# Where the operands of the dense products begin in SBUF: rows without a pad, tensors at multiples of 512 bytes

## The reference, cut to what matters

```python
def first_block(x, mem, ...):
    u = rms_norm(h, g_mix[l]) @ w_in[l]          # then two kinds of attention
    ...
    h = h + y @ w_out[l]
    h = h + cross_attention(rms_norm(h, g_cross[l]), rms_norm(mem, g_mem[l]), ...)
    a = jnp.square(jax.nn.relu(rms_norm(h, g_mlp[l]) @ w_up[l]))
    h = h + a @ w_down[l]

def _shift(z):
    return jnp.pad(z, ((0, 0), (1, 0), (0, 0)))[:, :-1]

def _rwkv7_mixer(h, r, k, v, mu_w, mu_a, w0, w1, w2, a0, a1, a2, ...):
    h_prev = _shift(h)                            # token t sees token t-1; token 0 sees zeros
    xw = h + (h_prev - h) * mu_w
    xa = h + (h_prev - h) * mu_a
    w = -jax.nn.softplus(-(w0 + jnp.tanh(xw @ w1) @ w2)...) - 0.5
    a = jax.nn.sigmoid((a0 + (xa @ a1) @ a2)...)
```

## The kernel before

| operand | begins at (before) | steps from row to row | begins at (after) |
|---|---|---|---|
| h, row k | 32 + 32 k | 4128 | 0 |
| u, row k | 288 + 32 k | 4128 | 0 |
| y, row k | 0 | 4096 | 0 |
| ul and hid in arena, row k | 384 | 4096 | 0 |
| w_hi, w_lo, part k | 0 | 512 | 0 |

## Time and profile before

### The profile page before, as it was taken

How to read it: one execution, slowest core, us unless ns; L and a number is a source line. 1 busy time by engine, 2 the same in 40 slices (tenths; PEclk the granted TensorE clock), 3 DMA queues, 4 the chain that set the end, 5 groups by cost and what they waited for, 6 DMA issues and landing times.

```text
span 2386.9 us, 35554 instructions
## 1 busy us (share of the span) xinstructions
PE 2287.9 (96%) x14900; PEld 1784.5 (75%) x14900; DVE 1176.7 (49%) x1498; ACT 866.1 (36%) x1524; POOL 546.9 (23%) x244
## 2 busy tenths in 40 slices
PE   7999999998999999999999999999999999999997
PEld 4777766666787877778888888888676777778885
DVE  6777746768565554532122122123416566467654
ACT  4444357767444222231121131133325422354321
POOL 2322212121211222222222222222131133222221
PEclk9999999999999999999999999999999999999999
DMA  3211101113131100111111111112221011100022
GB/s 129 79 45 53 54 27 36 54 45 124 62 124 45 35 28 27 44 44 53 45 44 53 44 48 49 44 53 80 80 69 31 18 36 37 46 18 13 4 107 80
DMA packets 37279, 125.88 MB, mean 53 GB/s; under 512 B 3856, under 2 KB 4368, under 8 KB 36752
## 3 DMA queue, kind: packets, MB, share of 16 engines
q1 hardware_dynamic: 30864, 103.30, 13.4%
q10 hardware_dynamic: 6272, 20.49, 2.3%
HBM read 114.34 MB, written 8.91 MB: 52 GB/s over the span
## 4 chain that ended last, share of the span: by engine, by line
PE 84%; DVE 9%; ACT 5%; issue 2%; DMA 1%; ACTq 0%; DVEq 0%
PE PS L182 22%; PE PS L184 21%; PE PS L183 21%; PE PS L2012 2%; PE PS L748 1%; PE PS L771 1%; PE PS L1196 1%; PE PS L898 1%; PE PS L933 1%; PE PS L915 1%; DVE arena L1017 1%; PE PS L316 1%; PE PS L1633 1%; DVE arena L397 1%; PE PS L1493 1%
## 5 line engine op out<-in xcount | busy, mean ns | idle before, releaser
L182 PE MATMUL PS<-u_r,w_hi 128*128 128x512 f32 x1280 | 522.7, 408 | 18.0 <-DVE y_r L192 5.4
L184 PE MATMUL PS<-u_r,w_lo 128*128 128x512 f32 x1280 | 507.3, 396 | 0.0
L192 POOL TENSOR_TENSOR w_lo<-w_raw,w_hi 128x1024 fp32r<-128x1024 f32 x143 | 364.1, 2546 | 587.4 <-ACT w_hi L188 581.4
L183 PE MATMUL PS<-arena_r,w_hi 128*128 128x512 f32 (+1 forms) x1152 | 439.4, 381 | 0.0
L231 POOL TENSOR_TENSOR w_hi<-w_raw,const 128x1024 fp32r<-128x1024 f32 x77 | 153.1, 1989 | 1143.3 <-PE PS L182 1093.8
L182 PEld LDWEIGHTS PS<-u_r,w_hi 128*128 128x128 f32 x1280 | 241.7, 189 | 82.8 <-DVE arena_r L192 6.5
L184 PEld LDWEIGHTS PS<-u_r,w_lo 128*128 128x128 f32 x1280 | 241.6, 189 | 57.4
L183 PEld LDWEIGHTS PS<-arena_r,w_hi 128*128 128x128 f32 x1152 | 216.9, 188 | 43.1 <-issue 0.7
L182 PE MATMUL PS<-h_r,w_hi 128*128 128x512 f32 x512 | 210.5, 411 | 4.0 <-DVE u_r L405 3.7
L184 PE MATMUL PS<-h_r,w_lo 128*128 128x512 f32 x512 | 202.9, 396 | 0.0
L183 PE MATMUL PS<-y_r,w_hi 128*128 128x512 f32 x512 | 202.0, 395 | 0.0
(11 more groups left out here) (399 smaller groups left out, 3573.0 us busy)
## 6 DMA issues: line engine op xcount, KB each, us to landing
w_raw<-in_w SPq DMA_DIRECT2D x174, 512.0 KB, 3.5
arena<-in_w SPq DMA_DIRECT2D x10, 512.0 KB, 4.7
h<-in_xT ACTq DMA_DIRECT2D x1, 4096.0 KB, 15.4
u<-parked_stream ACTq DMA_DIRECT2D x1, 4096.0 KB, 13.0
out<-arena SPq DMA_DIRECT2D x16, 256.0 KB, 2.0
parked_stream<-h ACTq DMA_DIRECT2D x6, 512.0 KB, 2.6
h<-in_xT SPq DMA_DIRECT2D x8, 256.0 KB, 7.3
h<-in_xT ACTq DMA_DIRECT2D x8, 256.0 KB, 9.1
```

The source lines that it names most:

```text
L182: first = pe.matmul(out, a[0], b[0], start=start, stop=False)
L183: pe.matmul(out, a[0], b[1], start=False, stop=False)
L184: return first, pe.matmul(out, a[1], b[0], start=False, stop=stop)
L192: return e.tensor_tensor(out, x, hi_part.bitcast(F), ALU.subtract)
```

## The change

Rows of h and u lose the pad and are 1024 words. h, u, y and arena are placed at multiples of 512 bytes; `small` and `ada` move behind arena. The shifted product of the first half of the tokens is cut in two: its first two columns are streamed from a small new tensor `edge` (two parts, high and low; 8 rows of two words, a zero and token 0), and the other 510 columns from h and u, words 1 to 510 of the row, into columns 2 to 511 of the bank. DVE fills `edge` ahead of its other work in `wa_dve`; PE waits for it. The two clearing instructions at the start go.

```diff
-        def with_rounded(name, shape):
+        def with_rounded(name, shape, align=512):
...
-            t = ctx.enter_context(nc.sbuf_tensor(name, shape, F, align_bytes=64))
+            t = ctx.enter_context(nc.sbuf_tensor(name, shape, F, align_bytes=align))
...
-        h_all, h_r = with_rounded("h", [P, KC, PAD + T])
-        u_all, u_r = with_rounded("u", [P, KC, PAD + T])
+        h_all, h_r = with_rounded("h", [P, KC, T])
+        u_all, u_r = with_rounded("u", [P, KC, T])
...
-        small = sb("small", [P, 64])
-        ada = sb("ada", [P, 24])
...
         arena, arena_r = arena_t[:, :], arena_rt[:, :]
+        small = sb("small", [P, 64])
+        ada = sb("ada", [P, 24])
+        edge = sb("edge", [P, 2, KC, 2], R)
...
         def in_u(k, lo, hi):
-            return u_r[:, k, PAD + lo:PAD + hi]
+            return u_r[:, k, lo:hi]
...
         def lora_down_pe(pe, h):
...
             if h == 0:
                 pe.wait_ge(S("gl_y_ready"), 1)
+                pe.wait_ge(S("edge_ready"), 2)
...
                 product(pe, bank(0), (rest_hi[:, k, :], rest_lo[:, k, :]), u_two(k, lo, hi), k == 0, False)
-                m = product(pe, bank(0), (mu_hi[:, k, :], mu_lo[:, k, :]), u_two(k, lo - 1, hi - 1), False, k == KC - 1)[1]
+                mu = (mu_hi[:, k, :], mu_lo[:, k, :])
+                if h == 0:
+                    product(pe, bank(0)[:, 0:2], mu, (edge[:, 0, k, :], edge[:, 1, k, :]), False, False)
+                    m = product(pe, bank(0)[:, 2:HALF], mu, u_two(k, 1, hi - 1), False, k == KC - 1)[1]
+                else:
+                    m = product(pe, bank(0), mu, u_two(k, lo - 1, hi - 1), False, k == KC - 1)[1]
...
         def wa_dve(dve):
+            dve.wait_ge(*split_ready("u2"))
+            dve.memset(edge[:, :, :, :].bitcast(F), 0.0).then_inc(S("edge_clear"), 1)
+            dve.wait_ge(S("edge_clear"), 1)
+            for x, source in enumerate((h_r, u_r)):
+                dve.tensor_copy(edge[:, x, :, 1:2], source[:, :, 0:1].bitcast(F)).then_inc(S("edge_ready"), 1)
             dve.wait_ge(S("wa_in"), 32)
...
-            dve.memset(u_r[:, :, 0:PAD].bitcast(F), 0.0)
-            dve.memset(h_r[:, :, 0:PAD].bitcast(F), 0.0)
...
-            act.dma_start(uT[:, :, PAD:], park_d[:, 0:KC, :]).then_inc(S("parked"), 16)
+            act.dma_start(uT, park_d[:, 0:KC, :]).then_inc(S("parked"), 16)
```

More of the change, by code:

```diff
@@ L147, in vcol @@
             return vec[:, VEC[name][0] + j:VEC[name][0] + j + 1]
-        h_all, h_r = with_rounded("h", [P, KC, PAD + T])
-        u_all, u_r = with_rounded("u", [P, KC, PAD + T])
+        h_all, h_r = with_rounded("h", [P, KC, T])
+        u_all, u_r = with_rounded("u", [P, KC, T])
         y_all, y_r = with_rounded("y", [P, KC, T])
-        hT, uT, yT = h_all[:, :, PAD:PAD + T], u_all[:, :, :], y_all[:, :, :]
+        hT, uT, yT = h_all[:, :, :], u_all[:, :, :], y_all[:, :, :]
         NS = 4
@@ L161, in program @@
         arena, arena_r = arena_t[:, :], arena_rt[:, :]
+        small = sb("small", [P, 64])
+        ada = sb("ada", [P, 24])
+        edge = sb("edge", [P, 2, KC, 2], R)
         def U(k, lo=0, hi=T):
-            return uT[:, k, PAD + lo:PAD + hi]
+            return uT[:, k, lo:hi]
         def pair(high, low):
@@ L170, in in_u @@
         def in_u(k, lo, hi):
-            return u_r[:, k, PAD + lo:PAD + hi]
+            return u_r[:, k, lo:hi]
         def in_h(k, lo, hi):
-            return h_r[:, k, PAD + lo:PAD + hi]
+            return h_r[:, k, lo:hi]
         def in_y(k, lo, hi):
@@ L2763, in _ @@
             pre = (in_(hT), lambda k: gpre[:, k:k + 1], f_rs, "fin")
-            u2 = (in_(uT[:, :, PAD:]), in_h, in_u, pre, lambda k: ada[:, k:k + 1])
+            u2 = (in_(uT), in_h, in_u, pre, lambda k: ada[:, k:k + 1])
             for q in range(14):
@@ L2988, in u2_split @@
             def u2_split(h, ks):
-                split_act(act, "u2", h, in_(uT[:, :, PAD:]), in_h, lambda k: [norm_out("fin", k, h)], ks, shift=lambda k: ada[:, k:k + 1])
+                split_act(act, "u2", h, in_(uT), in_h, lambda k: [norm_out("fin", k, h)], ks, shift=lambda k: ada[:, k:k + 1])
             for q in range(14):
```

## The result

| | before | after |
|---|---|---|
| median of the runs beside each other (4 and 4) | 2395.94 us | 2367.98 us |
| lowest and highest | 2384.31 to 2396.93 | 2366.30 to 2374.37 |
| ratio, with 95% interval | | 0.9889 (0.9873 to 0.9904) |
| profiled execution, span | 2386.9 us | 2372.6 us |
| its time | not recorded | 2374.37 us |

The kernel became some 27 us faster (1.1%; 0.0111 x 2395.9 = 26.6 by the ratio, 23 to 30 by its interval, 28.0 between the medians); 17.5 had been forecast, 2379 us, in a range of 2363 to 2399. The profiled execution of after is the slowest of its four; only 1.8 us of its time lie outside the span.

What follows compares the result with a forecast made beforehand. The prediction took PE's matmul spacing to bound the kernel: MLP -10.2, other products -9.7, edge matmuls +2.4, together -17.5 us from the 2396.3 us median, giving 2379 us, in a range of 2363 to 2399 us.

Steps and rivals of the forecast that it cites:

- What bounds the kernel, and the cause: PE, busy 96% of the span; distance between operands' beginnings sets matmul spacing, with a floor of 226.7 ns.
- Rival 1: Everywhere: beginnings don't matter, so only the edge matmuls' +2.4 us is left, 2399 us; chance 0.11.
- rival 3: All streams: in step is the bad place, 395 ns a matmul, 19.7 us slower, 2416 us; chance 0.07.
- MLP, -10.2 us: Four up stages each 1.70 us and four down stages each 0.84 us shorter, all on the path.
- The other products, -9.7 us: Outside the MLP, 4080 wide matmuls: 2720 gain 4.3 ns each, 11.7 us, of which 9.7 on the path.
- 0.83: Share of the products outside the MLP taken to lie on the path, 821 / 987, giving 9.7 of 11.7 us.
- Rival 2: Outside the MLP nothing gains, as only long runs settle: -10.2 + 2.4 = -7.8 us, 2388 us; chance 0.18.
- Settling: In product pieces, spacing comes down to the floor only after some matmuls; 8 of every 24 spent on it.
- The edge matmuls, +2.4 us: 24 two-column matmuls on PE, priced at 0.098 us each from a one-column row with the same weight load.
- pieces whose first third is uneven: Sign of being right, outside the MLP: a piece's first third is uneven and its rest even.
- DVE and the transfers, nothing: DVE's small instructions fall in idle time, PE's wait for edge is over early, u's reload is covered: no cost.
- The sum: -10.2 - 9.7 + 2.4 = -17.5 us on the 2386.9 us span; median 9.4 us above it carried over: 2379 us.

Runs made afterwards that it cites:

- the second and the third: Profiles of the changed kernel run again unchanged: medians 2370.07 us (0.9900 to before) and 2369.36 us (0.9890), profiled spans 2367.8 and 2366.0 us.
- the second profile of before: The kernel before, unchanged, profiled again: measured 2394.25 us, span 2392.5 us, MLP down stages 89.60 us and up stages 88.75 us.
- before's three spans: Profiled spans of the unchanged kernel before: 2386.9, 2392.5 and 2391.2 us; the second and third profiles measured 2394.25 and 2393.01 us.

## Why the prediction was right, and where it was not

**What bounds the kernel, and the cause.** Right. PE's spacing set the time, the distances between the beginnings set the spacing, and not the multiple of 512 (all moved by 96 bytes). Rival 1 falls with the kernels that move nothing but an address and lose up to 35 us; rival 3 with 389 ns in every in-step stream.

**MLP, -10.2 us.** Right to the row: 87.04 us against a forecast of some 87.0 us for both stages, on the path throughout. It holds for before's first profile; against the second, with its down stages at 89.60, it is 10.2 + 6.8 = 17.1 us.

**The other products, -9.7 us.** The total came out about right, by luck: two factors were too pessimistic and the third too hopeful. The excess outside the MLP was 20.4 us, 5.0 ns for each of 4080, not 4.3; and 4.9 of it are left, a quarter, where I let a third stay unsettled. So 15.5 us left PE's spacing, not 11.7. Of this the spans show, after the MLP's 10.2 and with 2.6 us for the edges added back, 14.3 - 10.2 + 2.6 = 6.7 us in the first profile of after, and likewise 11.5 and 13.3 in the second and the third (spans of 19.1 and 20.9 us less): 10.5 in the mean, against 9.7; that is 0.68 of the 15.5, where I had taken 0.83. Rival 2 (nothing outside the MLP) falls with that.

**Settling.** It exists, but not in after. With arena at 384, where this stretch has stream and weights at 384 and its surroundings stand at 0, the first matmuls are uneven, and then all is even:

```profile
794.12 0.39 PE L185 MATMUL PS<-arena_r 128*128 128x512 f32 x1
...
795.96 0.39 PE L184 MATMUL PS<-arena_r 128*128 128x512 f32 x1
796.18 0.39 PE L185 MATMUL PS<-arena_r 128*128 128x512 f32 x1
796.41 0.39 PE L186 MATMUL PS<-arena_r 128*128 128x512 f32 x1
```

Eight steps of 230 ns to 795.96, then 226 or 227. What came ahead is carried along for a while. I took the third of a piece from a kernel in which the neighbours were out of step, and put it on one in which they are not; that part of the forecast ("pieces whose first third is uneven") did not come.

**The edge matmuls, +2.4 us.** Right in size, 2.6 to 2.7 by the trace. One-column matmuls with the same weight load were the right row: 0.098 us there, 0.11 here; what I had not seen is that a part of it falls on the wide matmul behind.

**DVE and the transfers, nothing.** Right. After on DVE: the three small instructions on `edge`, and what line 1985 (1973 before) still waits for, answering to the earlier trace rows:

```profile
L1977 DVE MEMSET edge<- x1: 85/85/85, 2036.2 to 2036.2; 128x32 f32 x1
L1980 DVE CAST edge<-h_r x1: 172/172/172, 2036.3 to 2036.3; 128x8 fp32r<-128x8 f32 x1
L1980 DVE CAST edge<-u_r x1: 165/165/165, 2036.4 to 2036.4; 128x8 fp32r<-128x8 f32 x1
...
  DMA arena<-in_lora: 14.8, 1
```

0.42 us, ahead of 14.8 us of idle time, 31 us before PE asks for `edge`. The reload of u took 12.5 us instead of 13.0.

**The sum.** This is the step that failed: "The median stands 9.4 us above that span; I carry the difference over". It took 9.4 us for something that the change doesn't touch. Only 1.8 us lie outside a span. The rest was the difference between before's profiled execution and its usual one, and a part of this is made by the same streams out of step: the second profile of before has 6.6 us more excess than the first, 6.8 of slower down stages being the cause, and after has only one pattern, so that these go too. Span against span the forecast was good: 17.5 us, and 14.3, 19.1 and 20.9 measured against the first profile of before, 18.1 in the mean. Against the mean of before's three spans (2390.2) it is 21.4 us. The median of 19 other runs of before, less 1.8 us outside, is another 3 us above that mean, 2395.02 - 1.8 = 2393.2. By the estimate above ten of these 19 runs, the median one among them, had the slower pattern; only a profile shows the pattern itself.

## What to carry to other kernels

Where short-spaced matmuls stream from several tensors, put all streams and the weights at one remainder modulo 512 bytes, row by row (a pad of 8 words per row undoes it), and check it by the stages' times: here it was worth 1.1%, and one tensor out of place gave more than half of that back (arena), or all of it (the weights). Modulo 256 may do, by one execution of one kernel. A profiled execution that is faster than the median is a question to be answered before anything is added to it: the difference may be the very thing that the change removes. A few columns treated apart are not free: each group of three matmuls of two columns, with a weight load each, cost 0.33 us here.

## What the runs showed of the hardware

The spacing of two matmuls depends on where their operands begin relative to each other, weights included, and on what ran ahead: 226.67 ns in step, up to 233.3 ns (89.60 us / 384) in steady patterns out of step. Why the distance counts, no run shows. In step a 512-column product takes 544 cycles of 2.4 GHz, and no steady stretch went under that. The Trainium skill, "TensorE: Matmul & The Clock Gate", Back-to-back issue gap, gives 216 ns for 512 columns as an isolated gap, and about 131 ns in a stream of loads and matmuls. The traces agree with neither: 226.67 ns is the least of them.

Out of step, the same instructions have more than one steady pattern, fixed for all four rounds of an execution; the next one can have another (87.89 and 89.60 us).

PE's clock can fall behind a pause. Windows of after around a wait of 5.5 us that ends at 890.2 us:

```profile
884.00:888.00 4.00, 0.72 (x4) 0.26 (x2) 4.00 (x2) 0.34 (x1) 3.54 (x2) 0.97 0.00 0
888.00:892.00 4.00, 1.76 (x7) 1.60 (x8) 3.02 (x8) 2.54 (x8) 0.00 (x0) 0.50 0.46 135
892.00:896.00 4.00, 4.00 (x14) 3.17 (x13) 2.16 (x5) 0.97 (x4) 0.00 (x0) 0.68 0.00 0
896.00:900.00 4.00, 3.89 (x20) 3.10 (x19) 3.31 (x9) 2.62 (x8) 0.00 (x0) 1.00 0.00 0
```

0.50 is the lower of the two levels, 1.2 GHz, and it stays for a part of the busy time behind. Not each pause does so in each execution. The first profile of after against its second, from 600 to 620 us:

```profile
600.00:620.00 20.00, 17.31 (x105) 11.82 (x104) 16.39 (x15) 14.03 (x18) 5.34 (x2) 0.87 0.09 27
```

```profile
600.00:620.00 20.00, 16.56 (x108) 11.73 (x107) 16.39 (x15) 13.21 (x17) 5.34 (x2) 1.00 0.09 27
```

By the same sum as above after's three profiles lost 20.4, 15.8 and 18.8 us to it. It is not the whole of the few microseconds by which they differ: the third lost 3.0 us more than the second and has a span 1.8 us shorter.
